# Attention scores of both branches issued as one pair per head, masks last, with two sets of score banks in token tiles 0 to 3

## What is computed

```python
    s = jnp.einsum('bgrqd,bgnd->bgrqn', qi, ck) * scale            # 63 compressed keys
    p_c = masked_softmax(s, cmp_end[None, :] <= t[:, None])
    o_c = jnp.einsum('bgrqn,bgnd->bgrqd', p_c.astype(dt), cv)
    ...                                                            # top 16 of 16 blocks: every key up to t
    s = jnp.einsum('bgrqd,bgqkd->bgrqk', qi, ksel) * scale
    p_s = masked_softmax(s, smask[:, :, None])
    o_s = jnp.einsum('bgrqk,bgqkd->bgrqd', p_s.astype(dt), vsel)
    s = jnp.einsum('bgrqd,bgkd->bgrqk', qi, kwi) * scale           # window of 512 tokens
    p_w = masked_softmax(s, wmask)
    o_w = jnp.einsum('bgrqk,bgkd->bgrqd', p_w.astype(dt), vwi)
    o = gates[..., 0:1] * o_c + gates[..., 1:2] * o_s + gates[..., 2:3] * o_w
```

## Time and profile before

| what | value |
|---|---|
| median of 3 runs | 1595.13 us (1593.61 to 1596.15) |
| the profiled execution | 1594.84 us |
| its span, first to last instruction | 1593.0 us |
| granted TensorE clock, mean | 0.992 |
| PE busy | 1554.4 us, 98% of the span |
| DVE busy | 894.0 us, 56% |
| ACT busy | 537.2 us, 34% |
| attention stage | from about 365 to 650 us |

### The profile page before, as it was taken

The page is one execution under the profiler, slowest core; times in us unless marked ns, Lnnn a source line. Parts: engine busy times, 40 slices in busy tenths (PEclk is TensorE's granted clock), DMA queues, the critical chain, the costliest instruction groups (busy, mean ns, idle before and its releaser), DMA issues.

```text
span 1593.0 us, 21511 instructions
## 1 busy us (share of the span) xinstructions
PE 1554.4 (98%) x8238; PEld 1261.9 (79%) x8238; DVE 894.0 (56%) x1561; ACT 537.2 (34%) x936; POOL 79.7 (5%) x126
## 2 busy tenths in 40 slices
PE   8999999998899999999999999999999999999997
PEld 6888888897666666788888888888888888888885
DVE  7832456446777676443455555656555565556332
ACT  6112222246777677422212211222112221223221
POOL 0111222220000000000000000000000000000000
PEclk9999999998999999999999999999999999999998
DMA  6433342380000000601211111121111111122011
GB/s 230 133 106 126 100 145 95 115 257 18 25 18 14 14 1 10 242 1 42 78 40 58 61 40 40 40 79 40 40 40 55 64 40 40 40 80 106 27 40 40
DMA packets 53239, 110.57 MB, mean 69 GB/s; under 512 B 13104, under 2 KB 22320, under 8 KB 53168
## 3 DMA queue, kind: packets, MB, share of 16 engines
q1 hardware_dynamic: 45744, 85.47, 16.1%
q0 software_dynamic: 7424, 24.12, 4.5%
HBM read 89.65 MB, written 19.92 MB: 69 GB/s over the span
## 4 chain that ended last, share of the span: by engine, by line
PE 95%; DVE 2%; issue 2%; ACT 1%; DMA 0%; DVEq 0%; POOLq 0%; POOL 0%; SPq 0%; ACTq 0%
PE ps L1520 29%; PE ps L1139 15%; PE ps L1141 15%; PE ps L1140 15%; PE ps L1246 5%; PE ps L1425 5%; PE ps L1382 2%; PE ps L1383 2%; PE ps L1507 1%; PE ps L1291 1%; PE ps L1239 1%; PE ps L1144 1%; PE ps L1386 1%; PE ps L1205 1%; PE ps L1380 0%
## 5 line engine op out<-in xcount | busy, mean ns | idle before, releaser
L2069 DVE TENSOR_TENSOR h<-h,ps 128x512 f32<-128x512 f32 x336 | 224.4, 686 | 137.8 <-PE ps L1141 136.2
L1520 PE MATMUL ps<-htl,wuh 128*128 128x512 f32 x672 | 206.9, 389 | 0.0
L1520 PE MATMUL ps<-hth,wul 128*128 128x512 f32 x672 | 206.9, 389 | 0.0
L1520 PE MATMUL ps<-hth,wuh 128*128 128x512 f32 x672 | 206.8, 389 | 0.0
L1139 PE MATMUL ps<-wh,xth 128*128 128x512 f32 (+1 forms) x448 | 175.2, 391 | 7.6 <-DVE wl L1654 7.6
L1141 PE MATMUL ps<-wh,xtl 128*128 128x512 f32 (+1 forms) x448 | 169.2, 378 | 0.0
L1140 PE MATMUL ps<-wl,xth 128*128 128x512 f32 (+1 forms) x448 | 168.7, 377 | 0.0
L1520 PEld LDWEIGHTS ps<-hth,wul 128*128 128x128 f32 x672 | 126.1, 188 | 26.2
L1520 PEld LDWEIGHTS ps<-hth,wuh 128*128 128x128 f32 x672 | 126.1, 188 | 26.2
L1520 PEld LDWEIGHTS ps<-htl,wuh 128*128 128x128 f32 x672 | 126.1, 188 | 26.2
L1083 ACT ACTIVATE ffh<-ffa 128x1024 fp32r<-128x1024 f32 x22 | 23.3, 1061 | 358.3 <-DVE ffa L2096 358.3
(11 more groups left out here) (249 smaller groups left out, 2593.6 us busy)
## 6 DMA issues: line engine op xcount, KB each, us to landing
wuraw<-in_w_up SPq DMA_DIRECT2D x44, 512.0 KB, 4.9
wraw<-in_w_in SPq DMA_DIRECT2D x48, 256.0 KB, 3.3
proj_d<-stage POOLq DMA_DIRECT2D x48, 256.0 KB, 2.3
wdraw<-in_w_down SPq DMA_DIRECT2D x22, 512.0 KB, 3.6
rin<-proj_d POOLq DMA_DIRECT2D x20, 256.0 KB, 4.7
xraw<-in_xt SPq DMA_DIRECT2D x16, 256.0 KB, 6.0
owraw<-in_w_out SPq DMA_DIRECT2D x8, 512.0 KB, 5.5
h<-in_x SPq DMA_DIRECT2D x1, 4096.0 KB, 16.6
```

The source lines that it names most:

```text
L1520: mm = nc.tensor.matmul(ps[:, 2 * part + half, :], w_, x_[:, k, half * 512:(half + 1) * 512], start=(k == 0 and i == 0), stop=(k == NK - 1 ...
L2069: nc.vector.tensor_tensor(hh, hh, ps[:, 4 + o_ % 4, :], ALU.add).then_inc(dn_add, 1)
```

## The change

`qk` is split into products and masks and called for a pair of items, so that TensorE runs, for each head, the products of both branches, and then the masks of both. The pair is issued after each odd slot; before, one item was issued after each slot. The maximum of both items is taken by VectorE at the head of the even slot. ScalarE runs both exponentials at the end of the odd slot in tiles 0 to 3; in tiles 4 to 7 it runs them within the even slot, one half way through it and one at its end. In tiles 0 to 3, where an item takes one bank, heads take banks 0 and 2 or 1 and 3 in turn, and products wait for exponentials four items back instead of two, save where the compressed scores share bank 3: item 1 of a view waits for all exponentials up to the last of the view before, item 3 for `csub`.

```diff
+        def apart(t):
+            return 4 if t < WIN_T else 2
+        def score_bank(t, i):
+            r_, br = divmod(i, 2)
+            return 2 * br + (r_ % 2 if t < WIN_T else 0)
...
+            def exp_places(n, length):
+
+                v, i = divmod(n, 2 * RG)
+                if v >= NV:
+                    return {}
+                if v // G < WIN_T:
+                    return {length: [i - 1, i]} if i % 2 else {}
+                if i % 2:
+                    return {}
+                if i == 0:
+                    return {length: [0, 1]}
+                return {(length + 1) // 2: [i], length: [i + 1]} if length > 1 else {length: [i, i + 1]}
...
             for n, slot in enumerate(slots):
-                for st in slot:
+                at_ = exp_places(n, len(slot))
+                for m, st in enumerate([*slot, ("end",)]):
+                    for i in at_.get(m, ()):
+                        exponentials(n // (2 * RG), i)
                     {"split_q": q_split_high, "turn_q": q_turned, "turn_p": p_high, "turn_ret": ret_high,
                      "close": nsa_high}.get(st[0], skip)(st)
-                if n < 2 * RG * NV:
-                    exponentials(*divmod(n, 2 * RG))
...
-            def qk(v, i):
+            def qk_products(v, i):
...
-                if n >= 2:
+                if n >= apart(t):
+                    pe.wait_ge(exp_done, n - apart(t) + 1)
+                if i == 1 and t < WIN_T and n >= 2:
                     pe.wait_ge(exp_done, n - 1)
                 if i == 1 and v:
                     pe.wait_ge(csub_done, CSUB0 + v)
+                if i == 3 and t < WIN_T:
+                    pe.wait_ge(csub_done, CSUB0 + v + 1)
...
+            def qk_masks(v, i):
+
+                t, (r_, br) = v // G, divmod(i, 2)
+                far = br and t >= WIN_T
+                at = (t - (max(0, t - WIN_T) if br else 0)) * P
+                if far:
+                    nc.tensor.matmul(ps[:, 2, 0:P], ident_b[:], far_b, start=False, stop=True)
+                mm = nc.tensor.matmul(ps[:, score_bank(t, i) + at // 512, at % 512:at % 512 + P], ident_b[:], diag_b,
+                                      start=False, stop=not far)
+                if far:
+                    c0 = P + r_ * HD
+                    mm = nc.tensor.matmul(ps[:, 3, c0:c0 + HD], ident_b[:], cmp_b[:, t], start=False, stop=True)
                 mm.then_inc(qk_done, 1)
+
+            def qk_pair(v, r_):
+                for br in range(2):
+                    qk_products(v, 2 * r_ + br)
+                for br in range(2):
+                    qk_masks(v, 2 * r_ + br)
...
-            qk(0, 0)
+            qk_pair(0, 0)
...
-                if n + 1 < 2 * RG * NV:
-                    qk(*divmod(n + 1, 2 * RG))
+                if n % 2 and n + 1 < 2 * RG * NV:
+                    qk_pair(*divmod((n + 1) // 2, RG))
...
             for n, slot in enumerate(slots):
                 behind = n // 2 - 1
                 due = 0 <= behind < RG * NV
-                if n < 2 * RG * NV:
+                if n % 2 == 0 and n < 2 * RG * NV:
                     row_max(*divmod(n, 2 * RG))
+                    row_max(*divmod(n + 1, 2 * RG))
                 if n % 2 == 0 and due:
                     v_, head = divmod(behind, RG)
                     inverted = invert_sum(v_, head)
```

More of the change, by code:

```diff
@@ L938, in exponentials @@
                     act.wait_ge(tr_full, turns_of["turn_p", v - 2, len(key_tiles(v - 2)) - 1] + 1)
[L939 removed]
+                at = score_bank(t, i)
+                s_, pr = ps[:, at:at + 2, :].rearrange("p a n -> p (a n)"), prob[:, v % 2, r_]
                 m, q = n % 4, n // 2 % 4
@@ L1359, in qk @@
                     pe.wait_ge(csub_done, CSUB0 + v)
+                if i == 3 and t < WIN_T:
+                    pe.wait_ge(csub_done, CSUB0 + v + 1)
+                if i == 2 and v == 0:
+                    pe.wait_ge(cvc_done, CVC0 + 1)
                 q_ = aqt[:, v % 2, r_ * P:(r_ + 1) * P]
@@ L1365, in qk @@
                     w = min(512, width - c)
-                    bank = 2 * br + c // 512
+                    bank = score_bank(t, i) + c // 512
                     at = w0 * P + c
[L1368 to L1374, removed]
+                    if br and c:
                         two = ps[:, 3:5, :].rearrange("p a n -> p (a n)")[:, 0:2 * c0].rearrange("p (b n) -> p b n", b=2)[:, :, 0:P]
@@ L1379, in qk @@
                             pair = bass.AP(k_, first, [[CK + 3 * HD, P], [gap, 2], [1, P]])
-                            mm = nc.tensor.matmul(two, q_, pair, start=k_ is keys_s, stop=False)
+                            nc.tensor.matmul(two, q_, pair, start=k_ is keys_s, stop=False)
                     else:
+                        ends = c + w < width and not br
                         nc.tensor.matmul(ps[:, bank, 0:w], q_, aks[:, br, g_, at:at + w], start=True, stop=False)
[L1383 to L1388, removed]
+                        nc.tensor.matmul(ps[:, bank, 0:w], q_, akx[:, br, g_, at:at + w], start=False, stop=ends)
                 if i == 1 and t < WIN_T:
@@ L1394, in qk @@
                         nc.tensor.matmul(sc_, qc, ckx[:, g_ * NCMP:g_ * NCMP + HD], start=False, stop=False)
-                        mm = nc.tensor.matmul(sc_, ident_b[:], cmp_b[:, t], start=False, stop=True)
-                mm.then_inc(qk_done, 1)
+                        nc.tensor.matmul(sc_, ident_b[:], cmp_b[:, t], start=False, stop=True)
+            def qk_masks(v, i):
[9 more added lines that the diff above has]
+                    mm = nc.tensor.matmul(ps[:, 3, c0:c0 + HD], ident_b[:], cmp_b[:, t], start=False, stop=True)
+                mm.then_inc(qk_done, 1)
+            def qk_pair(v, r_):
[3 more added lines that the diff above has]
+                    qk_masks(v, 2 * r_ + br)
             def p_turn(st):
@@ L1890, in row_max @@
                 m = n % 4
-                s_ = ps[:, 2 * br:2 * br + 2, :].rearrange("p a n -> p (a n)")
+                at = score_bank(t, i)
+                s_ = ps[:, at:at + 2, :].rearrange("p a n -> p (a n)")
                 if br == 0:
@@ L1899, in row_max @@
                 c_ = cmpst[:, v % 2]
-                scores = s_[:, 5 * P:5 * P + RG * HD].rearrange("p (r n) -> p r n", r=RG)[:, :, 0:NCMP]
+                scores = ps[:, 3, P:P + RG * HD].rearrange("p (r n) -> p r n", r=RG)[:, :, 0:NCMP]
                 maximum = mark(nc.vector.reduce_max(c_[:, C_MAX], scores, AX_X, negate=True))
```

## The result

The changed kernel took 1624.89 us (median of 5 runs, 1624.16 to 1628.92) against 1595.13 us before: ratio 1.0192, 95% interval 1.0181 to 1.0203. That is slower, well beyond the noise and as forecast, but by 29.8 us where the sum said 14.7. The profiled execution took 1624.65 us, with a span of 1622.9.

The account below looks back on a forecast made before the run. TensorE's waits were taken to decide, with VectorE also mattering in tiles 0 to 3. 8.8 + 3.9 + 0.3 - 2.4 - 3 + 4.1 + 3 = +14.7 us on 1594.84 gave 1609 us, range 1599 to 1618.

Parts of the forecast that it names:

- (a): Tiles 4 to 7, change of views: item 0's mask comes about 0.7 us later; +8.8 us together with (b).
- (b): Change of views, tiles 4 to 7: window's maximum ahead of head 3 delays normalising 0.74 us; +8.8 us with (a).
- (c): Tiles 4 to 7: item 7's exponentials ahead of the last copies make last outputs wait; +3.9 us, plus +0.3 in view 8.
- (d): Fewer switches between bf16 masks and 32-bit products, 0.10 us a head for 24 heads: -2.4 us, bounds 0 and -5.
- (e): Tiles 0 to 3, second bank set against item 1's lateness: -3 us in tiles 0 to 2, +4.1 in tile 3.
- (f): Longer PE waits make the clock fall two times more in the stage: +3 us, bounds -1.5 and +9.
- The 0.45 at view 9: Time view 9's third turn had waited, taken off its 1.43 us delay at the change of views.
- the `retl` wait that was counted as gone: Third turn's wait for the retention transpose's bank, said to go at changes of views, leaving only (a) at three.
- net -0.5 for each of six views: Tiles 0 to 2: earlier window product and lifted waits outweigh the later first turn; -3 us, bounds -8 and +3.
- the clock falls at nearly every change: Rival, slower still: six more stretches at the lower clock give 1616 us; chance 16%.

Follow-up runs that it names:

- `a_fill`: Changed kernel plus 3 to 11 products without use on TensorE ahead of the first turn of eleven views: 1613.38 us.
- `a_norm_first`: Changed kernel, but at each change of views VectorE finishes head 3 of the old view before both maxima of the new one: 1599.47 us.
- `a_fill_exp`: `a_fill` with item 7's exponentials put back behind the copies in tiles 4 to 7: 1612.65 us.
- `a_mended`: Changed kernel, pairs kept, with head 3 normalised first, compressed products behind the masks in tiles 0 to 3, retention transpose late in its view: 1595.75 us.
- `b_two_norm_ret_mask`: `b_two_norm` with the retention transpose late in its view and the window item's far mask behind the joint products in tiles 4 to 7: 1586.44 us.
- `b_two_sets`: Kernel before, item by item, with only the two sets of score banks in tiles 0 to 3: 1591.49 us.
- `a_fill_comp`: `a_fill` with item 1's twelve compressed products and their wait behind the pair's masks in tiles 0 to 3, and fewer fillers: 1610.87 us.
- `a_mended_exp`: `a_mended` with item 7's exponentials back at the end of their view, behind the copies: 1587.84 us.
- `b_two_norm`: `b_two_sets` with head 3 of the old view finished on VectorE before the new view's maximum: 1591.12 us.
- `b_two_norm_ret_mask_fill`: `b_two_norm_ret_mask` plus products without use ahead of each item from the third on in views 0 to 3: 1586.46 us.
- `b_two_fill`: `b_two_sets` plus products without use ahead of each item from the third on in views 0 to 3: 1590.68 us.
- `b_two_norm_ret_fill`: `b_two_norm` with the retention transpose late in its view, plus products without use ahead of items in views 0 to 3: 1588.03 us.

## Why the direction was right and the size was not

The stage's +29.4 us against the steps of the prediction. Tiles without falls are read from `a_fill`; what the clock cost is the rest.

| step | forecast | shown | from |
|---|---|---|---|
| (a), (b), (c), (d): tiles 4 to 7 | +10.6 | +11.1 | 202.6 less 193.0, and 1.5 for the fall of the earlier trace rows, which `a_fill` doesn't have |
| (e), tile 3 | +4.1 | +4.0 | 33.3 less 29.3 |
| (e), tiles 0 to 2 | -3 | about +2 | 69.4 less 65.0, less 2.6 for 6.8 us at the low level in view 3 at 0.38 |
| (f), the clock | +3 | about +12.5 | what is left of 29.4; by 34.0 us more at 0.38 it is 12.9 |

**(a) and (b) held.** The forecast was 0.7 and 0.74 at a change of views; into view 12 they are 0.71 and 0.73, and into views 8 to 11 the first turn comes 1.44 to 1.48 later behind the pair's start, where 1.43 was said. (The 0.45 at view 9 is 0.29 by the earlier trace rows, which moves the sum by 0.2.) `a_norm_first` shows that this chain sets the end. The weak part was the cover: nothing covered it, as said, but the `retl` wait that was counted as gone only hid behind it.

**(c) held in place, and its size was too high.** The outputs of views 8 to 10 wait 2.9 us in three stops, forecast 3.9:

```profile
499.67 0.65 PE L1464 MATMUL ps<-ptf,cv 63*64 63x256 f32 x4 [1.53 <-ACT ptf L972]
521.30 0.65 PE L1464 MATMUL ps<-ptf,cv 63*64 63x256 f32 x4 [0.63 <-ACT ptf L972]
545.43 0.65 PE L1464 MATMUL ps<-ptf,cv 63*64 63x256 f32 x4 [0.76 <-ACT ptf L972]
```

A fourth stop of 0.59 us (666.84) was missed: view 15 has no next pair behind which the last copies hide. But (c) also pays back there. Without it (`a_fill_exp`) the part from the query transposes of view 14 on is 1.7 us longer, so that of the 3.1 us some 1.5 are left, and 0.7 to 1.2 in the time. About 6 us is what it is worth in `a_mended`, where it meets the late retention transpose. Since (d) was not tried in the changed kernel either, that the four terms together come within 0.5 us of the forecast may be luck in part.

**(d) held for the part that was tried.** The step from mask to joint product saved 1.6 us in the 32 window items of `b_two_norm_ret_mask`, 0.05 each, as said; the prediction counted 24 of them. By the formula of the Trainium skill ("TensorE: Matmul & The Clock Gate", section "Back-to-back issue gap"), which has no term for what went before and is given there for a product by itself, it would have saved nothing; the 1.6 us disagree. The rest of the 2.4, one entry into key products fewer, was not tried by itself.

**(e) failed in tiles 0 to 2.** The prediction said that the second set of banks would pay back more than item 1's lateness. `b_two_sets` shows that the sets pay, 3 to 4 us; what failed is the term "net -0.5 for each of six views". It took the earlier window product as 1 us paid back, but that product is item 1's, whose wait for the exponentials of the old view the change keeps. At views 4 and 5 that wait did nearly go (0.93 to 0.18 us at view 5); at views 2 and 3 it grew, from 0.67 and 0.84 to 1.08 and 1.42 us, and it comes in front of the first turn, in series with the turn's own. `a_fill_comp`, which takes this away, makes the part up to view 7 5.2 us shorter, of which about 1.3 (3.4 us at 0.38) is the clock. With the order mended (`a_mended_exp`) the stretch is 59.0 us, 6.0 under before.

**(f) failed most.** The mechanism was in the text, and the rival "the clock falls at nearly every change" was the case that came true, but it was priced as six falls more, 9 us in all. There were nine more in the stage, six of them in tiles 1 to 3, where the forecast had two more in all; 34.0 us more at the low level are ten stretches of 3.4 us, and about 12.5 us for them is 1.25 each, under the 1.5 that was said. So the count failed, not the price. (The prediction also says that the clock fell once before; it fell twice, the other being the 13.7 us in tile 0.) With (e)'s own sign wrong the rival's 1616 was 9 us short as well. The prediction itself put waits of 2.0 to 2.8 us at several changes of views; in the trace seven of the nine waits of 2.0 us and more have a fall with them or right behind. A weight of 16% was too little for it, and the range, whose upper bound was 1618, left out that (e) and (f) hang on the same waits and go wrong together.

## What to carry to other kernels

Where the first work of a new unit and the last work of the old one meet on an engine, finish the old one first if the busiest engine waits for it: one edit of order on VectorE was worth 25 us in the pairs, and nothing in the kernel with single items, where `retl` stood behind it. When a change lengthens waits of TensorE, count each as a possible fall of the clock (here nine of fourteen had one), and price it where TensorE carries the stage; waits and falls are one risk, not two. And an edit that shortens one wait is worth its length only when the one next in line is known: `b_two_norm` and `a_fill_exp` gave about 1 us or less: in the one `retl` stood right behind, in the other the end of the stage became longer.

## What the runs showed of the hardware

- Each us at the low level cost 0.38 us in a stage that TensorE carries most of the time (`a_fill`). The Trainium skill ("TensorE: Matmul & The Clock Gate", section "Terms") puts the penalty at the time throttled times (1 - K/N), a half; an estimate by that is 15.3 us for the 30.6, and 11.5 were measured. Why it is less is open in part: over the ten falls behind that of tile 0 PE was busy for 34.7 of 37.4 us, and `a_fill` waits 1.9 us for copies ahead of a turn where the changed kernel has 0.2.
- In view 3 the low level cost 0.2 us at a mean of 0.86 and 3.0 us at 0.68, by the three traces above: a short stretch went into PE's slack, a longer one did not.
- Products without use of 128 x 512 ahead of a wait kept the clock at its upper level, in `a_fill` from view 4 on and in `b_two_norm_ret_mask_fill` in the whole stage, where they left the time as it was. In `b_two_fill` and `b_two_norm_ret_fill` falls came behind the views that have them (421.7 and 527.5; 423.2).
- The mean clock differs from run to run of one and the same program, and with it come two levels of the time some 4 us apart in several of the kernels here (`b_two_sets`: 1590.5 to 1591.5 at 0.991 and 0.992, 1594.5 to 1595.7 at 0.989). Where in the program it differs is shown only by traces of kernels that are alike up to tile 3, as those of view 3 above. With products ahead of each item in views 0 to 3 (`b_two_fill`) the runs lie within 3.1 us, with no second level.
